# A fused attention and mLSTM block: the probability transposes move from the middle of each unit to the head of the block of small products

## What is computed

```python
scores = jnp.einsum('bcqkgd,bcskd->bckgqs', qc, kb).astype(jnp.float32) * (ATT_HEAD_DIM ** -0.5)
scores = jnp.where(valid[None, :, None, None, None, :], scores + bias, -jnp.inf)
probs = jax.nn.softmax(jnp.concatenate([scores, sink], axis=-1), axis=-1)[..., :-1]
out = jnp.einsum('bckgqs,bcskd->bcqkgd', probs.astype(vb.dtype), vb)
...
mix = jnp.concatenate([rms_norm(att, g_attn_out[l]), rms_norm(mh, g_mlstm_out[l])], axis=-1)
x = x + mix @ w_out[l]
h2 = rms_norm(x, g_ffn[l])
x = x + (jax.nn.silu(h2 @ w_gate[l]) * (h2 @ w_up[l])) @ w_down[l]
```

## Time and profile before

| What | Value |
|---|---|
| Median of 3 runs | 1007.28 us (1007.04 to 1007.73) |
| The profiled execution's own time | 1006.92 us |
| Its span, first to last instruction | 1005.2 us |
| TensorE (PE) busy | 998.6 us |
| VectorE (DVE) busy | 648.3 us |
| ScalarE (ACT) busy | 438.1 us |
| GpSimd (POOL) busy | 692.1 us |
| Matmuls of the probability transposes (L983) | 64 in 8 groups, 228.5 to 295.2 us |

### The profile page before, as it was taken

The page is one execution under the profiler, slowest core; times in us unless marked ns, Lnnn a source line. Parts: engine busy times, 40 slices in busy tenths (PEclk is TensorE's granted clock), DMA queues, the critical chain, the costliest instruction groups (busy, mean ns, idle before and its releaser), DMA issues.

```text
span 1005.2 us, 13420 instructions
## 1 busy us (share of the span) xinstructions
PE 998.6 (99%) x4960; PEld 830.7 (83%) x4960; DVE 648.3 (64%) x777; ACT 438.1 (44%) x904; POOL 692.1 (69%) x545
## 2 busy tenths in 40 slices
PE   8999999999999999999999999999999999999998
PEld 7899888888888888888888888888888888888887
DVE  4259526558862678885748577674748586674585
ACT  7545145547750657524334352433334252433440
POOL 0128768826675515996887787887878788788792
PEclk9999999999999999999999999999999999999999
DMA  7113212141032002112112112112112212211213
GB/s 240 59 53 93 64 44 69 59 157 33 22 126 64 21 11 74 53 42 84 43 42 84 42 42 81 46 42 75 52 43 67 61 42 57 70 42 48 83 59 137
DMA packets 71017, 66.00 MB, mean 66 GB/s; under 512 B 5288, under 2 KB 53544, under 8 KB 70952
## 3 DMA queue, kind: packets, MB, share of 16 engines
q1 hardware_dynamic: 69944, 64.64, 20.8%
q10 hardware_dynamic: 1008, 0.50, 0.2%
HBM read 60.42 MB, written 4.21 MB: 64 GB/s over the span
## 4 chain that ended last, share of the span: by engine, by line
PE 96%; DVE 2%; ACT 1%; issue 1%; DMA 0%; SPq 0%; DVEq 0%; ACTq 0%
PE banks L812 30%; PE banks L814 29%; PE banks L813 29%; PE banks L832 1%; PE banks L1008 1%; PE banks L905 1%; PE banks L983 1%; ACT prob L1511 1%; PE banks L970 1%; PE banks L917 0%; DMA x_in<-in_x 0%; PE banks L927 0%; PE banks L881 0%; PE banks L870 0%; DVE af_lo_apart L2069 0%
## 5 line engine op out<-in xcount | busy, mean ns | idle before, releaser
L742 POOL TENSOR_TENSOR wr_lo<-wr_raw,wr_hi 128x512 fp32r<-128x512 f32 x231 | 319.3, 1414 | 26.8 <-ACT wr_hi L1329 21.6
L736 POOL TENSOR_TENSOR wr_raw<-wr_raw,wr_raw 128x512 f32<-128x512 f32 x132 | 193.3, 1469 | 132.5 <-PE banks L814 75.8
L812 PE MATMUL banks<-hf_hi,wr_hi 128*128 128x512 f32 x616 | 239.9, 390 | 0.0
L814 PE MATMUL banks<-hf_hi,wr_lo 128*128 128x512 f32 x616 | 239.7, 389 | 0.0
L813 PE MATMUL banks<-hf_lo,wr_hi 128*128 128x512 f32 x616 | 239.7, 389 | 0.0
L1329 ACT ACTIVATE wr_hi<-wr_raw 128x512 fp32r<-128x512 f32 x231 | 136.7, 625 | 164.8 <-POOL wr_raw L736 107.5
L2151 DVE TENSOR_TENSOR x<-banks,x 128x1024 f32<-128x1024 f32 x138 | 168.8, 1224 | 51.6 <-PE banks L814 35.2
L812 PE MATMUL banks<-w_hi,actT_hi 128*128 128x512 f32 (+1 forms) x448 | 173.1, 386 | 0.0
L814 PE MATMUL banks<-w_hi,actT_lo 128*128 128x512 f32 (+1 forms) x448 | 168.4, 376 | 0.0
L813 PE MATMUL banks<-w_lo,actT_hi 128*128 128x512 f32 (+1 forms) x448 | 168.2, 375 | 0.0
L812 PEld LDWEIGHTS banks<-hf_hi,wr_hi 128*128 128x128 f32 x616 | 115.6, 188 | 24.4 <-issue 0.3
(11 more groups left out here) (204 smaller groups left out, 1191.3 us busy)
## 6 DMA issues: line engine op xcount, KB each, us to landing
wr_raw<-in_w_up SPq DMA_DIRECT2D x46, 256.0 KB, 3.2
wr_raw<-in_w_gate SPq DMA_DIRECT2D x44, 256.0 KB, 3.3
wr_raw<-in_w_down SPq DMA_DIRECT2D x44, 256.0 KB, 3.2
w_raw<-in_w_in SPq DMA_DIRECT2D x32, 256.0 KB, 3.3
w_raw<-in_w_out SPq DMA_DIRECT2D x16, 256.0 KB, 2.6
x<-in_x SPq DMA_DIRECT2D x8, 512.0 KB, 6.5
out<-x SPq DMA_DIRECT2D x16, 256.0 KB, 2.1
x_in<-in_x SPq DMA_DIRECT2D x7, 512.0 KB, 4.4
```

Of the source, the lines that this page charges most:

```text
L736: nc.gpsimd.tensor_tensor(wr_raw[slot(q, f)][:, :], wr_raw[slot(q, a)][:, :], wr_raw[slot(q, b)][:, :], ALU.subtract).then_inc(wsum, 1)
L742: nc.gpsimd.tensor_tensor(wr_lo[s][:, :], wr_raw[s][:, :], wr_hi[s][:, :].bitcast(F32), ALU.subtract).then_inc(wf_lo, 1)
L812: nc.tensor.matmul(ps, x_hi, wh, start=first, stop=False, skip_group_check=more)
L814: return nc.tensor.matmul(ps, x_lo, wh, start=False, stop=last, skip_group_check=more)
```

## The change

The call of att_prob_transposes is taken out of both kinds of unit and made once, at the head of the block of small products of the same U, ahead of the query transposes. The function itself and its waits stay as they are, as do the programs of all other engines.

```diff
@@ in unit(U)
-                    if k == K // 2 and U >= 4 * T + 4:
-                        att_prob_transposes(U - 4 * T - 4)
@@ in out_unit(U)
                 for part, done in ((0, wa_done), (1, wb_done)):
-                    if part == 1 and U - 4 * T - 4 < T:
-                        att_prob_transposes(U - 4 * T - 4)
@@ in the loop over U, behind the unit
                 s = U - 4 * T
+                if 0 <= s - 4 < T:
+                    att_prob_transposes(s - 4)
                 if s == 1:
                     pe.wait_ge(c_ready, T)
                     pe.wait_ge(mh_ready, T)
                 if 0 <= s - 1 < T:
                     att_transposes(s - 1)
```

## The result

The changed kernel takes 1011.15 us (median of 6 runs, 1010.35 to 1011.93), the kernel before, timed beside it, 1007.32 us (6 runs). The ratio is 1.004, 95% interval 1.003 to 1.005: slower by 3.8 us, where I forecast 1.7 and a range that ended at 1011.0.

What follows compares the result with a forecast made beforehand. The prediction took TensorE to bound the kernel: two block stalls of 0.9 us less 0.1 gained make +1.7 us on the median 1007.28, so 1009.0 us, range 1007.5 to 1011.0.

Steps and rivals of the forecast that it cites:

- TensorE is the bound and nothing behind the attention stage absorbs a loss.: Whole kernel: TensorE busy 998.6 of 1005.2 us, so whatever it loses or saves shows at the end.
- The move itself costs TensorE nothing.: Eight transposes cost 0.88 us inside a unit and 0.87 in a block; eight groups gain 0.1 us.
- Blocks 42 and 43 lose 0.9 each.: Value products directly behind the transposes wait for DVE's copy; 0.9 us each, 1.8 together (1.7 to 1.9).
- Block 41 and blocks 37 to 40: no loss.: Other work hides the copies: scores leave 0.14 us margin in block 41, 0.5 in blocks 37 to 40.
- What is late next.: Work behind DVE's later copy: bank-1 addition hidden by 1.3 us, scores of block 41 1.25 later; no loss added.
- Units 36 to 43 as long as unit 44: Expected sign in the trace: without transposes inside, these units last like unit 44, 5.34 us, with no wait inside.
- The durations of DVE.: DVE's operation times taken from the kernel before, such as copy 0.69 us, normalising to addition 0.61, addition 0.75.
- No cost: POOL gets its reciprocal up to 1.7 us later; its weight slice for unit 40 is still 2.8 early.
- draw: Block 42: exponentials of tile 7 free ACT for its copy at 290.6 us, transposes end at 290.52; narrowest place.
- Rival 1: More or longer block stalls: blocks 41 and 42 (+2.5 us), perhaps four query blocks too (+3.7); 1009.5 to 1011, chance 0.15.
- Rivals 2 and 3: Copies hidden in blocks 42 and 43, 1007.2 to 1008, chance 0.10; large matmuls gain in one piece, 1005, chance 0.03.
- rival 4: TensorE's clock falls at the two stalls, half speed for one unit, +5.3 us; 1014, chance 0.04.

Runs made afterwards that it cites:

- e3: Against the kernel before, only tiles 6 and 7 (blocks 42 and 43) get the moved transposes; 1009.06 us, ratio 1.0014.
- e8: Against the kernel before, only tiles 0 to 4 moved, and DVE makes tile 7's scaled queries ahead of the row maxima; 1007.84 us, ratio 1.0001.
- e4: The changed kernel with DVE making tile 7's scaled queries ahead of the row maxima; 1009.21 us, ratio 1.0018 to the kernel before.
- e1: Against the kernel before, only tiles 0 to 3 (blocks 36 to 39) moved; 1008.28 us, ratio 1.0008.
- e5: The kernel before, nothing moved, POOL making the high part of four weight slices (units 36 to 39) twice; 1008.9 us, ratio 1.0013.
- e6: The changed kernel with POOL normalising only 2 of 128 columns of each of its probability blocks; 1009.1 us, ratio 1.0016 to the kernel before.
- e2: Against the kernel before, only tiles 4 to 7 (blocks 40 to 43) moved; 1009.84 us, ratio 1.0024.

## Why the prediction was wrong

- *TensorE is the bound and nothing behind the attention stage absorbs a loss.* Right. The stretch's 4.03 us show up as 3.8 in the medians, and from block 44 on no new wait appears. TensorE's busy time was to be unchanged and grew by 1.2 us; 0.95 of that is the start-up of the last section.
- *The move itself costs TensorE nothing.* Right. Blocks 37 to 39 follow each other at 9.75 us by their query transposes (253.15 - 243.40) where it was 9.78, a gain of 0.03 a group; I had taken 0.01.
- *Blocks 42 and 43 lose 0.9 each.* Block 43: 0.88; e3 with both alone, 0.89 and 0.87. The term holds. In block 43 the restart came 0.11 behind DVE's copy (303.27 against 302.47 + 0.69 = 303.16), inside the bounds of 0.05 and 0.14. The weights did not run ahead: their load began at 303.24, 0.08 behind the copy.
- *Block 41 and blocks 37 to 40: no loss.* Right, by -0.02 in the table and by e8.
- *"What is late next."* This step failed. It followed DVE's queue to x1_ready and to the scores, and never named the scaled queries behind them; it had "Units 36 to 43 as long as unit 44". It left out the wait of unit 40 on bank 1, where the kernel before had 0.20 us of slack (queries done at 268.59, part 1 at 268.85, less the release of 0.06). Both the 0.87 us that left the middle of unit 40 and DVE's 1.2 us fell on this slack. It cost 1.93 us (1.96 by e4), as much as the two stalls that I had found, and stood in the sum at nothing.
- *The durations of DVE.* I carried them over from before, and closed POOL's lateness with "No cost". (It was to be up to 1.7 us; my own two numbers, 272.9 and 271.4, give 1.5, and 1.6 was measured at block 39.) For the two 128x8 operations that was wrong: they can last until POOL's instruction ends, and POOL was moved against them. This made DVE's lateness at unit 40 (1.03 us of loss, e1) and 0.56 us of the exponentials' lateness at block 42 (in iteration 41 the row maxima operation took 1.26 us where it was 0.70), where my "draw" then turned into 0.3 us of loss. e5 and e6 show it in both directions.
- *Rival 1* foresaw the side and about the time (1009.5 to 1011), and the place of its third part, block 42. Its main term was elsewhere, so that the time came out at its upper end is luck. Rivals 2 and 3 are out: the copies are not hidden (0.89 and 0.87 in e3), and a unit in one piece gains 0.03. The clock (rival 4) stayed up: behind the longest stall, 1.62 us, the matmuls start 0.24 us apart at once (271.19, 271.43), the spacing of the upper level, 2.4 GHz. The rule of the Trainium skill on short idles (page "TensorE: Matmul & The Clock Gate", section "A second HAM failure mode: psum-queue depth-cycling") did not come into play with these three.

The stretch of the changed kernel holds 0.2 us more than those of e1 and e2 add up to (1.03 + 2.81 = 3.84). That is the slack of 0.20 us, which each run alone had to use up. It is worked out from the traces; no run sets the slack itself. What stays open is why block 36 takes 0.04 to 0.15 us longer in every kernel but the one before and e6, also where nothing is moved ahead of it.

## What to carry to other kernels

When a group of operations is moved on the bounding engine, list every wait of that engine behind the old and the new place with its slack, also those that concern other data: the moved work was also the time cushion of whatever waited behind it. Moving the reader of a copy next to its writer costs the whole copy with its two releases (0.9 us here), unless other work stands between. And carry over a duration only if its neighbours on the other engines stay where they were: a tiny VectorE operation on SBUF data can last until the end of the GpSimd instruction that it meets under way.

## What the runs showed that I had not expected

- The 128x8 operation of the row maxima on DVE lasts from 0.17 (e5) to 1.27 us (e8), for the same 8 elements a partition. Where it was held above, its end lies 0.02 us behind the end of a POOL instruction; where it was not (0.17 us, e5), it had begun 0.14 us ahead of POOL's. DVE's busy time rose by 4.7 us in the changed kernel with the same instructions; this operation has 3.3 of it (8.2 against 4.9 over its eight times) and the one behind it 1.5 (4.3 against 2.8).
- A TENSOR_SCALAR of 128x8 with one tensor input was held as well: 0.77 us in e5, ending 0.03 behind POOL's, where the changed kernel has 0.22.
- The start-up differs from run to run: block 36 begins its query transposes between 231.69 us (e4) and 233.37 us (the changed kernel), although nothing is changed ahead of it. In the profiled execution of the changed kernel the large matmuls of unit 0 still stood 0.43 us apart at 10.34 us, twice the spacing and so what the lower level, 1.2 GHz, would give, where those of the kernel before stood 0.23 apart, although the granted clock reads full from the first slice in both. The transposes in the middle of unit 0 begin at 12.38 us there and at 11.43 before. These 0.95 us are, to 0.01, what block 36 starts later.
